# Key forget sums by a fused DVE add-and-maximum from rows broadcast over the partitions, and value projections with exchanged operands, in a two-block transformer kernel

## The reference

```
hn = rmsnorm(h, g_mix);  rq, rk, rv, rg, fq, fk, fv, ff = split(hn @ w_in)
ret = retention(rotary(rq), rotary(rk), rv)              # 8 heads of 64
log_f = log_sigmoid(ff + b_forget);  F = cumsum(log_f)   # 8 heads
logits = fq.fk/8 + F[query] - F[key], causal
fox = softmax(logits) @ fv                               # 8 heads of 64
h = h + concat(silu(rg)*groupnorm(ret), fox) @ w_out
```

## Time and profile before

| | |
|---|---|
| median of 3 runs | 2082.29 us (2079.42 to 2082.4) |
| the profiled execution | 2085.64 us, of which its span 2083.8 us |
| PE busy | 98% of the span |
| DVE, ACT, POOL busy | 46%, 35%, 40% |
| retention loop, fox loop | about 184 to 235 us, about 236 to 308 us |
| everything after | 308 us to the end, dense units but for the other attentions |

### The profile page before, as it was taken

The page is one execution under the profiler, slowest core; times in us unless marked ns, Lnnn a source line. Parts: engine busy times, 40 slices in busy tenths (PEclk is TensorE's granted clock), DMA queues, the critical chain, the costliest instruction groups (busy, mean ns, idle before and its releaser), DMA issues.

```text
span 2083.8 us, 26839 instructions
## 1 busy us (share of the span) xinstructions
PE 2049.5 (98%) x9844; PEld 1682.6 (81%) x9844; DVE 955.3 (46%) x1249; ACT 722.2 (35%) x1093; POOL 842.6 (40%) x345
## 2 busy tenths in 40 slices
PE   8999999999999999999999999999999999999998
PEld 6788788878888878888888888887777888888886
DVE  3576865243888886622220153373442253222112
ACT  4334454343323222432322243224663343232221
POOL 2344323313544444344444434443223444444442
PEclk9999999999999999999999999999999999999998
DMA  5253212204655585232333325332213323233231
GB/s 202 89 154 103 78 59 84 74 31 139 207 189 191 191 284 189 81 101 91 101 94 98 97 75 152 113 99 81 62 61 91 91 81 101 92 99 100 91 101 60
DMA packets 66504, 233.26 MB, mean 112 GB/s; under 512 B 7552, under 2 KB 8832, under 8 KB 65920
## 3 DMA queue, kind: packets, MB, share of 16 engines
q1 hardware_dynamic: 65712, 231.11, 35.1%
q10 hardware_dynamic: 720, 1.15, 0.2%
HBM read 224.37 MB, written 2.10 MB: 109 GB/s over the span
## 4 chain that ended last, share of the span: by engine, by line
issue 63%; POOL 29%; PE 6%; POOLq 1%; DVE 0%; DMA 0%; ACT 0%; SPq 0%; DVEq 0%; ACTq 0%
POOL wlo L419 29%; PE bank L1727 2%; PE bank L1728 2%; PE bank L1729 2%; POOLq L418 0%; DMA raw<-units 0%; POOLq L425 0%; DVE h L1587 0%; PE bank L1628 0%; PE bank L1629 0%; ACT whi L448 0%; PE bank L1763 0%; DVE ssum L962 0%; PE bank L1634 0%; PE bank L1753 0%
## 5 line engine op out<-in xcount | busy, mean ns | idle before, releaser
L419 POOL TENSOR_TENSOR wlo<-raw,whi 128x1024 fp32r<-128x1024 f32 x341 | 842.4, 2471 | 1218.2 <-ACT whi L448 1218.2
L1628 PE MATMUL bank<-xh,whi 128*128 128x512 f32 x1680 | 660.9, 393 | 8.5 <-ACT whi L448 7.5
L1629 PE MATMUL bank<-xl,whi 128*128 128x512 f32 x1680 | 655.9, 390 | 0.0
L448 ACT ACTIVATE whi<-raw 128x1024 fp32r<-128x1024 f32 x343 | 362.0, 1056 | 642.1 <-PE bank L1634 356.4
L1634 PE MATMUL bank<-xh,wlo 128*128 128x512 f32 x1680 | 415.1, 389 | 0.0
L1628 PEld LDWEIGHTS bank<-xh,whi 128*128 128x128 f32 x1680 | 316.5, 188 | 78.7 <-ACT whi L448 8.6
L1629 PEld LDWEIGHTS bank<-xl,whi 128*128 128x128 f32 x1680 | 316.8, 189 | 65.3 <-issue 0.7
L1634 PEld LDWEIGHTS bank<-xh,wlo 128*128 128x128 f32 x1680 | 315.4, 188 | 65.9
L1727 PE MATMUL bank<-hh,whi 128*128 (+1 forms) x528 | 205.7, 390 | 1.9 <-POOL wlo L419 1.8
L1728 PE MATMUL bank<-hl,whi 128*128 (+1 forms) x528 | 205.4, 389 | 0.0
L1729 PE MATMUL bank<-hh,wlo 128*128 (+1 forms) x528 | 205.4, 389 | 0.0
(11 more groups left out here) (282 smaller groups left out, 2127.9 us busy)
## 6 DMA issues: line engine op xcount, KB each, us to landing
raw<-units SPq DMA_DIRECT2D x343, 512.0 KB, 3.5
ada_w<-ada_rows SPq DMA_DIRECT2D x72, 512.0 KB, 4.6
h<-x_t SPq DMA_DIRECT2D x8, 256.0 KB, 6.6
out_t<-h SPq DMA_DIRECT2D x8, 256.0 KB, 2.1
mem_in<-mem_t SPq DMA_DIRECT2D x1, 1024.0 KB, 12.1
turned_q<-proj SPq DMA_DIRECT2D x4, 256.0 KB, 5.7
dec<-decays SPq DMA_DIRECT2D x4, 256.0 KB, 4.7
turned_k<-proj SPq DMA_DIRECT2D x4, 256.0 KB, 4.1
```

What stands on the lines that cost most here:

```text
L419: pool.tensor_tensor(wlo[:, j % 2 * UNIT:(j % 2 + 1) * UNIT], raw[:, j * UNIT:(j + 1) * UNIT], whi[:, j % 2 * UNIT:(j % 2 + 1) * UNIT].bit ...
L448: act.activation(whi[:, v % 2 * UNIT:(v % 2 + 1) * UNIT], raw[:, slot * UNIT:(slot + 1) * UNIT], ACT.Copy).then_inc(hi_ready, 1)
L1628: mm(bank[:, 0:n], wh, chunk(rhs[0], t, n), start=t == 0, stop=False)
L1629: mm(bank[:, 0:n], wh, chunk(rhs[1], t, n), start=False, stop=False)
```

## The change

Four things change in the first 310 us:

- rv and fv are computed with exchanged operands (`value_units`): the activations are the stationary side and the weights (laid out anew on the host) the moving one, so the values come out with tokens on the partitions, in banks 4 to 7, and no transposes follow. ACT copies the banks with the norm factor of the token as its scale (`values_scale`); DVE's eight scalings of rv and fv are gone.
- The matmuls with `lt` and `rh`, and all that makes these two, are gone. `forget_sum` now writes -F of the eight heads to eight partitions (`neg_sums`).
- SP sends each of the eight rows to all 128 partitions, by a DMA from SBUF to SBUF that repeats its source: four heads (`sums_of_a`, partitions 0 to 3) between the loads of units 35 and 36, after `forget_sum`; four (`sums_of_b`, partitions 4 to 7) between the loads of units 39 and 40, after the last retention head, in whose values' place they go.
- For each fox head DVE does one operation per group that adds the row of sums to the scores in PSUM, writes the sum to SBUF (`p_fox` or `tmp`) and gives the row maximum. ACT takes the exponential in place in SBUF. PE writes the next head's scores once the maxima are there (`fox_max`) and no longer waits for the exponentials.

```
@@ sync
             turn(1, turned_k, proj, PR["rk"], 4)
+            def broadcast_sums(g):
+                for n in range(4):
+                    sp.dma_start(chunk(sums_of[g], n), neg_sums[4 * g + n:4 * g + n + 1, :].unsqueeze(1).to_broadcast([1, P, T])).then_inc(sums_in[g], 16)
+            u = units_to(u, 36)
+            sp.wait_ge(gate_dve, 3)
+            broadcast_sums(0)
+            u = units_to(u, 40)
+            sp.wait_ge(ret_pv, NRET)
+            broadcast_sums(1)
             u = units_to(u, lead)
@@ scalar
-            def values_copy(n, c0):
-                act.wait_ge(v_tr, QB * (n + 1))
+            def values_scale(name):
+                act.wait_ge(unit_used, L[name].u0 + 4)
                 for s in range(QB):
-                    act.activation(chunk(proj, c0 + s), banks[7 - s][:, :], ACT.Copy).then_inc(v_copied, 1)
+                    act.activation(chunk(proj, PR[name] + s), banks[4 + s][:, :], ACT.Copy,
+                                   scale=mix_root[:, s:s + 1]).then_inc(v_copied, 1)
...
-                        for q, b, o, w, po in k.groups[hd % len(k.groups)]:
-                            act.activation(p[:, po:po + w], banks[b][:, o:o + w], ACT.Exp,
+                        for q, _, _, w, po in k.groups[hd % len(k.groups)]:
+                            act.activation(p[:, po:po + w], p[:, po:po + w], ACT.Exp,
@@ vector
-                        for q, b, o, w, _ in k.groups[hd % len(k.groups)]:
-                            dve.reduce_max(mx[:, 4 * hd + q:4 * hd + q + 1], banks[b][:, o:o + w], AX.X).then_inc(k.s_max, 1)
+                        for q, b, o, w, po in k.groups[hd % len(k.groups)]:
+                            sums = chunk(sums_of[hd // 4], hd // 2 % 2 * 2 + q % 2)
+                            dve.tensor_tensor_reduce(k.p[hd % 2][:, po:po + w], banks[b][:, o:o + w], sums[:, 0:w], 1.0, -3e38,
+                                                     ALU.add, ALU.max, mx[:, 4 * hd + q:4 * hd + q + 1]).then_inc(k.s_max, 1)
...
-                scale_units("rv", to_proj(PR["rv"]), first=j, last=j + 1)
-                scale_units("fv", to_proj(PR["fv"]), first=j, last=j + 1)
...
-                dve.tensor_tensor_scan(forget, rb[0:8, :], tmp[0:8, 3 * T:4 * T], 0.0, ALU.mult, ALU.add).then_inc(gate_dve, 1)
+                dve.tensor_tensor_scan(neg_sums[0:8, :], ones[0:8, :], tmp[0:8, 3 * T:4 * T], 0.0, ALU.mult, ALU.add).then_inc(gate_dve, 1)
-            def forget_split():
-            def forget_right():
-            def right_rows(p):
@@ tensor
-            def values_to_tokens(c0, ready, b):
+            def value_units(name):
+                for j in range(4):
+                    u = L[name].u0 + j
+                    slot = u % 2
+                    pe.wait_ge(hi_ready, u + 1)
+                    for part in (range(3), (3,)):
+                        for kk in range(2):
+                            w0, c = slot * UNIT + kk * T, 2 * j + kk
+                            for s in part:
+                                if c == 0:
+                                    take(4 + s)
+                                x0 = c * T + s * P
+                                mm(banks[4 + s][:, :], xh[:, x0:x0 + P], whi[:, w0:w0 + T], start=c == 0, stop=False)
+                                mm(banks[4 + s][:, :], xl[:, x0:x0 + P], whi[:, w0:w0 + T], start=False, stop=False)
+                        if len(part) == 3:
+                            pe.wait_ge(lo_ready, u + 1)
+                        ...
+                    last.then_inc(unit_used, 1)
...
-                            pe.wait_ge(k.s_exp, 4 * hd)
+                            pe.wait_ge(k.s_max, 4 * hd)
...
-            values_to_tokens(PR["rv"], SCALED["rv"] + 4, 0)
-            values_to_tokens(PR["fv"], SCALED["fv"] + 4, 4)
...
-                for r, q, b, o, w, _ in groups:
-                    f0 = (c % 2 * 2 + r) * T
-                    mm(banks[b][:, o:o + w], lt[:, q * P:(q + 1) * P], rh[:, f0:f0 + w],
-                       start=False, stop=False, skip_group_check=True)
-
+                for _, _, b, o, w, _ in groups:
                     last = mm(banks[b][:, o + w - P:o + w], mask16[:, 0:P], mask16[:, 2 * P:3 * P],
                               start=False, stop=True, skip_group_check=True)
```

More of the change, by code:

```diff
@@ L95 @@
                   ("g_xk", 2), ("b_forget", 1), ("conv", 24), ("b_ada", 72), ("sinks", 16), ("eps", 1),
-                  ("one", 1), ("head_mask", 8)]:
+                  ("one", 1)]:
     VEC[_name] = (sum(n for _, n in VEC.values()), _n)
@@ L672, in _ @@
             act.wait_ge(setup_done, 1)
-            act.activation(rs[0:32, 0:1], lt[0:32, 0:1].bitcast(f32), ACT.Copy)
+            act.activation(rs[0:32, 0:1], ones[0:32, 0:1], ACT.Copy)
             act.wait_ge(vec_in, 16)
@@ L1334, in _ @@
                            ALU.mult).then_inc(ret_weighted, 1)
-                if s < 4:
-                    (forget_log, forget_sum, forget_split, forget_right)[s]()
+                if s < 2:
+                    (forget_log, forget_sum)[s]()
                 if s in (3, 5, 7):
@@ L1774, in head_sums @@
                     bank_free[4 + c] = [(hn_rstd, b + c + 1)]
-            def values_to_tokens(c0, ready, b):
-                for cs in (range(3), (3,)):
-                    pe.wait_ge(scaled, ready - 1 if len(cs) == 3 else ready)
-                    for s in range(QB):
-                        if len(cs) == 3:
-                            take(7 - s)
-                        for c in cs:
-                            last = nc.tensor.transpose(banks[7 - s][:, c * P:(c + 1) * P],
-                                                       proj[:, (c0 + c) * T + s * P:(c0 + c) * T + (s + 1) * P], ident)
-                        if len(cs) == 1:
-                            last.then_inc(v_tr, 1)
-                            bank_free[7 - s] = [(v_copied, b + s + 1)]
+            def value_units(name):
[14 more added lines that the diff above has]
+                            pe.wait_ge(lo_ready, u + 1)
+                        for kk in range(2):
+                            w0, c = slot * UNIT + kk * T, 2 * j + kk
+                            for s in part:
+                                x0 = c * T + s * P
+                                last = mm(banks[4 + s][:, :], xh[:, x0:x0 + P], wlo[:, w0:w0 + T], start=False, stop=c == 7)
+                    last.then_inc(unit_used, 1)
+                for s in range(QB):
+                    bank_free[4 + s] = [(v_copied, (4 if name == "rv" else 8) - 3 + s)]
             def all_banks_taken():
@@ L2021, in memory_values_unit @@
                     if half == 0:
-                        pe.wait_ge(fox.s_exp, 4 * NFOX)
+                        pe.wait_ge(fox.s_max, 4 * NFOX)
                         pe.wait_ge(gn_lo, 4)
@@ L2034, in _ @@
             for b in (0, 1, 2):
-                bank_free[b] = [(fox.s_exp, 4 * NFOX)]
+                bank_free[b] = [(fox.s_max, 4 * NFOX)]
             for b in (3, 4, 5):
@@ L2375, in lay_out @@
     assert units.shape == (UNITS, P, UNIT), units.shape
-    head_mask = np.zeros((P, 8), np.float32)
-    for r in range(P):
-        if r % 32 < 8:
-            head_mask[r, r % 32] = 1.0
     bf = np.zeros((P, 1), np.float32)
```

77 lines of the change are left out of this document (31 added, 46 removed).

## The result

| | before | after |
|---|---|---|
| median | 2080.86 us (4 runs, 2079.23 to 2082.4) | 2112.89 us (4 runs, 2111.8 to 2116.44) |
| ratio, 95% interval | | 1.0151 (1.0138 to 1.0164) |
| span of the profiled execution | 2083.8 us | 2114.6 us |

The change makes the kernel 32.0 us slower. I had forecast slower, but by 13.7 us (2096.0), with 2105 as the end of the range.

The account below looks back on a forecast made before the run. PE, busy 98% of the span, was taken to bound the kernel: 2082.3 - 3.1 - 3.8 = 2075.4, then + 8.4 + 10.6 - 0.8 + 2.4 = 2096.0 us; range 2073 to 2105.

Parts of the forecast that it names:

- the rate of the source: Broadcasts of the sums: four neighbouring source partitions give 27 GB/s, so 39 us per group of four transfers.
- the hidden case: Broadcasts: only the writing side limits, a group takes 3 us, unit 36 isn't late; 2075.4 us, 2072 to 2079; chance 0.27.
- The sign to look for: Profile after, broadcasts: some 10 us to landing for the first of a group, near 40 for the last.
- the sum without the transfers: Start of the retention loop and fox loop, all without the DMAs: 2082.3 - 3.1 - 3.8 = 2075.4 us.
- The value units: Start of the retention loop: transposes go (-3.5), a wait for ACT's copies comes (net +0.4); -3.1 us.
- the new fox loop: Fox loop: -1.1 us for heads 0 and 1, -0.45 for each of six steps; -3.8 us.
- The price that I set beside it: Fused operation in fox steps, by the skill's half-throughput rule: 1.7 us lost per step, some 9 for eight.
- PE wanted the unit at: Retention and fox loops: PE needs unit 36 at 226.6 and unit 40 at 271.2; delays +8.4 and +10.6 us.
- What is late then: Loads behind the broadcasts: unit 36 +8.4, unit 40 +10.6, waits covered -0.8, lower clock after pauses +2.4 us.
- the remark in brackets on ACT's decay loads: Retention step 4: ACT's two decay loads are slowed too, but PE waits longer for unit 36 anyway; no term.
- The step to 240.3: After unit 36 is ready at 235, 3.4 us for it and 1.3 for the last retention values; group b starts 240.3.
- Each us more per group adds two: Broadcasts: each further us that a group of four transfers takes adds two us to the kernel's time.

Follow-up runs that it names:

- rows_from_dram: Changed kernel with the rows of both groups' eight transfers read from a constant table in DRAM, not from neg_sums; 2076.63 us, ratio 0.9971.
- value_units_only: Kernel before with only the exchanged operands of the value units, ACT's scaling and the new rv and fv layout; 2078.44 us, ratio 0.9983.
- round_40_later: Changed kernel with group a's rows from a DRAM table and ACT's rounding of unit 40 moved from fox step 2 to 3; 2086.98 us, ratio 1.0036.
- no_second_reload: group_b_from_dram without ACT's two loads of decay tables in retention step 4; 2091.59 us, ratio 1.005.
- group_b_from_dram: Changed kernel with only group b's rows read from a constant table in DRAM, group a still from SBUF; 2095.25 us, ratio 1.0062.
- partitions_0_32: group_b_from_dram with each group a transfer reading two partitions of ones, 0 and 32, each copied to 64 partitions; 2097.31 us, ratio 1.0079.
- four_ports: group_b_from_dram with each group a transfer reading partitions 0, 32, 64 and 96 of ones, each copied to 32 partitions; 2076.73 us, ratio 0.9977.
- four_neighbours: group_b_from_dram with each group a transfer reading partitions 0 to 3 of ones, each copied to 32 partitions; 2095.83 us, ratio 1.007.

## Why the prediction was right in direction and wrong in size

ACT's roundings of units 36 and 40 in the trace of the kernel before, for the third point:

```profile
221.66 1.04 ACT L448 ACTIVATE whi<-raw 128x1024 fp32r<-128x1024 f32 x1
...
254.18 1.07 ACT L448 ACTIVATE whi<-raw 128x1024 fp32r<-128x1024 f32 x1
```

- *Right: the rate of the source.* 39 us per group forecast, 40.8 and 40.0 measured; 27 GB/s taken, 25.7 measured; the hidden case, the main rival, fell with it. The sign to look for, 10 us to the first landing and near 40 for the last, was read as 12.5 from issue for the first; the last landed 32.1 after its own issue, 40.8 after the first one's.
- *Right: the sum without the transfers.* 2075.4 forecast, 2076.6 and 2075.7 measured. The value units gave -3.2 where I had -3.1. From the retention scores to csilu rows_from_dram is 3.6 us shorter than the kernel before, and I had -3.8. But 1.2 of the 3.6 is the slow stretch of the earlier trace rows, gone in value_units_only too; the new fox loop itself (value_units_only against rows_from_dram) gave -2.3: -1.8 for six steps where I had -2.7, since two of the six are closed by other work, and -0.5 for heads 0 and 1 where I had -1.1. The fused group took 1.76 us with its read-outs (271.29 to 273.05), not 2.0, so the rule of the Trainium skill that spoke against it (Vector Engine (DVE) Microarchitecture Reference, "Points that are easy to get wrong") takes nothing from it here; the rule is about two sources in SBUF, and here one lies in PSUM. (The price that I set beside it doesn't add up either: 1.7 us for each of eight heads is 13.6, not some 9.) But the exponentials cost 0.17 more per head, and the scaling of the maxima took 0.57 in place of 0.17 where POOL's subtraction ran.
- *Wrong: "PE wanted the unit at".* The failed step is the last paragraph on the broadcasts, "What is late then", which takes the delay from PE's first matmul with units 36 and 40. ACT, in order, comes to their rounding 8 to 14 us before PE (in the old trace ACT rounds unit 36 at 221.66 and unit 40 at 254.18; PE starts them at 229.65 and 267.86), and what stands behind it on ACT, copies, roots and exponentials, is due for PE long before the unit is. The step has +8.4 and +10.6, with the -0.8 and +2.4 for the clock 20.6 in all. Measured: 18.6 for group a and 17.9 for group b, 36.5. The difference, 15.9, and the 1.2 by which rows_from_dram lies above 2075.4 make 17.1; from 2096.0 to 2112.9 it is 16.9. round_40_later shows it for group b: with ACT's rounding moved behind the copies, 7.5 of its 17.9 us go (6.7 of 20.1 in the middle part). For group a it is read from the timelines.
- *Wrong: the remark in brackets on ACT's decay loads.* I had seen them slowed and set them aside. They hold ACT for 7.7 us in the issue and DVE until they land. The price is small, since unit 36 is late behind them anyway: 1.6 us in the middle part of the traces, 3.7 by the medians of no_second_reload and group_b_from_dram.
- *Not in the sum:* group b started at 250.5 and not at 240.3, since group a's delay was larger; for group b that changes nothing by itself, as its cost is counted from the last retention head on. (The step to 240.3 has a slip of its own: 235 + 3.4 + 1.3 is 239.7, which would make the forecast 2095.4.)
- The range's upper end came from 43 us per group with the same wrong step. "Each us more per group adds two" had the price of a late unit right and its starting point wrong.

## What to carry to other kernels

When a transfer will be late, follow it to the engine that takes it first, in its own program order, and ask for every instruction queued behind that wait who needs it; the price is that of the first starved one, not of the unit itself. A DMA whose source is a few partitions is as slow as the ports that these lie on, whatever is free on the writing side: spread the source rows over blocks of four partitions, or let them go through DRAM. An engine that issues a DMA of its own while such a transfer fills the DMA engines can stand still too, as ACT did for 7.7 us. And before a difference of a few us between two kernels is put down to an edit, look whether it lies in the stretch that the edit changes.

## What the runs showed of the hardware that I had not expected

- Two source partitions as far apart as 0 and 32 share 27 GB/s, while 0, 4, 8 and 12 have 100 GB/s together.
- The issue of two DMAs of 256 KB by ACT took 7.72 us during the broadcast and 1.02 us without it (rows_from_dram), and it blocked ACT's next instruction. With a source of two or four partitions it took 2.30 us (partitions_0_32), 2.58 (four_ports) and 3.77 (four_neighbours).
- The share of busy DMA engines went with the number of source partitions when the source had several (0.12 for two, 0.22 and 0.24 for four), but was 0.90 and more for a source of one. A low share is not a sign of a free path: four neighbours moved 25 GB/s at a share of 0.22.
- After each long pause of PE its clock was granted lower: a mean of 0.72 from 237 to 250 us, behind a pause of 5.92, and 0.50, that is 1.2 GHz, from 293 to 297, behind the one of 19.95. Twelve score matmuls took 2.50 us in place of 1.45.
- Near the end, in the 10 us that begin 20 us before it, the granted clock was 1.00 in seven of the traces and 0.82 to 0.85 in the other seven, where PE started 37 or 38 matmuls in place of 45 or 46. The code there is the same in all. What decides between the two no run shows.
